# Two more expert steps in the second half's attention of a fused transformer and expert-retrieval block

## The reference

```python
def peer(h, w_q, sub_keys, expert_u, expert_v):
    q = jnp.einsum('bsd,dq->bsq', h, w_q).reshape(b, s_len, PEER_HEADS, 2, PEER_HALF)
    scores = jnp.einsum('bshpc,hpnc->bshpn', q, sub_keys).astype(jnp.float32)
    top_s, top_i = lax.top_k(scores, PEER_TOPK)
    ...
    best_s, best_pos = lax.top_k(cand_s, PEER_TOPK)
    best_i = jnp.take_along_axis(cand_i, best_pos, axis=-1)
    gate = jax.nn.softmax(best_s, axis=-1)
    ...
    def token_block(args):
        xb, ib, gb = args                      # 128 tokens, 128 experts each
        u = jnp.take(expert_u, ib, axis=0)
        act = jax.nn.gelu(jnp.einsum('td,tkd->tk', xb, u).astype(jnp.float32), approximate=False)
        vv = jnp.take(expert_v, ib, axis=0)
        return jnp.einsum('tk,tkd->td', (gb * act).astype(h.dtype), vv)
```

## Time and profile before

| | us |
|---|---|
| runs: lowest, median, highest | 2656.35, 2659.87, 3085.62 |
| profiled execution: time | 2648.0 |
| profiled execution: span of the core | 2646.3 |
| busy: PE, DVE, ACT, POOL | 2158.7, 1726.1, 659.7, 796.3 |

### The profile page before, as it was taken

The page is one execution under the profiler, slowest core; times in us unless marked ns, Lnnn a source line. Parts: engine busy times, 40 slices in busy tenths (PEclk is TensorE's granted clock), DMA queues, the critical chain, the costliest instruction groups (busy, mean ns, idle before and its releaser), DMA issues. The chain is left out here.

```text
span 2646.3 us, 26290 instructions
## 1 busy us (share of the span) xinstructions
PE 2158.7 (82%) x9024; PEld 1622.4 (61%) x9024; DVE 1726.1 (65%) x3624; ACT 659.7 (25%) x1537; POOL 796.3 (30%) x541
## 2 busy tenths in 40 slices
PE   8999999999999999998999988988555554544554
PEld 6787788888778777777888867877111211211221
DVE  4662110002327679687787676667999999999987
ACT  2103212102332421662320234532111111111110
POOL 0000000000001244234443322225754655645642
PEclk9999999999999999999999998889776777778776
DMA  6774334443245699798999974578999999999997
GB/s 256 289 286 130 135 112 159 146 157 116 97 170 225 268 381 419 261 332 344 415 421 412 400 267 176 191 269 328 422 421 422 421 421 421 421 395 421 421 422 298
DMA packets 114868, 798.33 MB, mean 302 GB/s; under 512 B 13328, under 2 KB 16528, under 8 KB 19248
## 3 DMA queue, kind: packets, MB, share of 16 engines
q0 software_dynamic: 74736, 540.57, 50.2%
q1 hardware_dynamic: 40000, 256.09, 26.3%
HBM read 790.27 MB, written 6.34 MB: 301 GB/s over the span
## 5 line engine op out<-in xcount | busy, mean ns | idle before, releaser
L588 PE MATMUL PS<-reg,ring 128*128 128x256 f32 x6016 | 1350.4, 383 | 28.1 <-ACT reg L1109 6.5
L588 PEld LDWEIGHTS PS<-reg,ring 128*128 128x128 f32 x6016 | 1142.5, 192 | 204.9 <-issue 35.9
L536 POOL DMA_INDIRECT uv<-in_expert_uv,experts x329 | 529.6, 1610 | 1610.6 <-DVE experts L1534 862.1
L1581 DVE SCALAR_TENSOR_TENSOR acc<-uv,coef,acc 128x1024 f32<-128x1024 f32 x261 | 335.3, 1285 | 9.5 <-DVE coef L1564 0.3
L563 PE MATMUL PS<-uv,spare 128*128 128x512 f32 x260 | 177.2, 832 | 169.9 <-ACT spare L1046 169.9
L1552 DVE CUSTOM_DVE_ANT_0 uv<-uv,h_tok 128x1024 f32<-128x1024 f32 x225 | 267.2, 1219 | 30.0 <-DMA uv<-in_expert_uv,experts 29.6
L563 PE MATMUL PS<-reg,spare 128*128 128x512 f32 x212 | 140.8, 814 | 118.6 <-ACT spare L1046 118.6
L563 PEld LDWEIGHTS PS<-uv,spare 128*128 128x128 f32 x260 | 64.9, 265 | 278.1 <-issue 278.1
L1053 ACT ACTIVATE acts<-dots 128x2 f32<-128x2 f32 (+2 forms) x194 | 39.4, 203 | 745.5 <-DVE dots L1552 689.2
L536 POOL DMA_INDIRECT reg<-in_expert_uv,experts x107 | 150.3, 1405 | 110.1 <-PE PS L563 39.9
L563 PEld LDWEIGHTS PS<-reg,spare 128*128 128x128 f32 x212 | 51.9, 259 | 206.3 <-issue 206.3
(11 more groups left out here) (265 smaller groups left out, 2102.4 us busy)
## 6 DMA issues: line engine op xcount, KB each, us to landing
ring<-in_weights SPq DMA_DIRECT2D x228, 1024.0 KB, 5.5
uv<-in_expert_uv,experts POOLq DMA_INDIRECT x329, 15.2
kv_half<-reg SPq DMA_DIRECT2D x1, 2052.0 KB, 11.1
reg<-kv_half SPq DMA_DIRECT2D x1, 2052.0 KB, 15.5
reg<-in_x_t SPq DMA_DIRECT2D x2, 1024.0 KB, 4.9
reg<-in_sub_t SPq DMA_DIRECT2D x2, 1024.0 KB, 5.0
toep<-rel_neg SPq DMA_DIRECT2D x16, 128.0 KB, 6.7
x_tokens<-reg SPq DMA_DIRECT2D x2, 1024.0 KB, 10.3
```

The lines of the kernel that those rows point to most:

```text
L536: gp.indirect_dma_start(UV[r], None, a["expert_uv_2"], bass.IndirectOffsetOnAxis(ap=experts[:, e % 256:e % 256 + 1], axis=0))\
L588: mm = pe.matmul(out_tile(n, t), w[:, t * P:(t + 1) * P], mv, start=first and k == 0, stop=last and k == KT - 1)
L1581: dve.scalar_tensor_tensor(acc[:, :], v, c, acc[:, :], ALU.mult, ALU.add).then_inc(acc_done, 1)
```

## The change

Two numbers are added to `MORE`, 6 and 14. A step (two slots) now also stands behind fill tile 6 (the seventh GC tile, item 10) and fill tile 14 (the seventh CP tile, item 20). `FIRST_PE` and `WIDE` move from 198 and 204 to 202 and 208. `STEPS`, the number of steps ahead of the tail, follows: from 99 to 101. The first slot of the tail is 202 instead of 198, and PE accumulates 152 slots instead of 154.

```diff
-FIRST_PE = 198
+FIRST_PE = 202
...
-NUV0, NUV1, WIDE = 7, 17, 204
+NUV0, NUV1, WIDE = 7, 17, 208
...
-MORE = (2, 10, 18)
+MORE = (2, 6, 10, 14, 18)
```

## The result

The changed kernel took 2672.02 us (median of 8 runs, lowest 2663.33), the kernel before 2657.0 beside it (lowest 2647.66). One run of each, 3809.62 and 3085.62 us, was slow (the first at a granted clock of 0.549) and is not in the ratio. The ratio is 1.0057, 95% interval 1.0039 to 1.0075: a loss of about 15 us, between 10 and 20, against a forecast of +10.5. The profiled execution took 2668.49 us with a span of 2666.7, 20.4 longer than before.

What follows compares the result with a forecast made beforehand. It took PE, with DMA nearly full, to bound the stretch from 1215 to 1500 us and gathers the tail. Terms -10.0, +10.3, +6.9, +3.3 gave +10.5: 2658.5 against 2648.0, 2670 on the median, range 2650 to 2688.

Steps and rivals of the forecast that it cites:

- Tail, -10.0: Tail, paced by the gathers: two steps are four slots less at 2.49 us each, -10.0 us.
- Attention, +10.3: Second half's attention: late combines behind tiles 6 (4.3) and 14 (6.5), less 2.5 for a moved routing, plus 2.0 clock; +10.3 us.
- Ahead of WO, +6.9: Attention projection's end: a routing now behind AP1 delays merges WO waits for; 5.4 us more waiting, 1.5 clock; +6.9 us.
- UP2 and UP10 at nothing: Routings landing at UP2 and UP10: PE's evacuations are ACT's and PE waits for nothing there; 0 us.
- DN10, +1: Routing ahead of the residual at DN10: up to 3.5 us late, but PE is late by then; +1 us.
- Mixers, +3.6: Mixers: a routing arrives ahead of the last mLSTM product, where PE already waits 3.69 us; +3.6, between 0 and 5.6.
- -1.3: WO2: a routing leaves it, behind which PE waits 2.59 us; -1.3 us, between 0 and -2.6.
- Q2 to V2, nothing: Stretch from Q2 to V2: no change in length, 0 us.
- The attention absorbs the steps: Rival, chance 0.22: DVE's 44.5 us idle takes the steps; attention +2, projection +4, tail -10; -4 us in all.
- The backlog grows: Rival, chance 0.13: DVE does not catch up between clusters; attention +19, projection +8, others +6, tail -7.5; +26 us.
- The clock stays low: Rival, chance 0.02: stalls keep PE at the lower rate for most of the attention; +59 us there, over 2% slower.
- A table switch holds ACT longer than its load: Rival, chance 0.03: four added switches each hold ACT 1.28 us more; attention 5.1 us more, +15.6 in all.

Runs made afterwards that it cites:

- the spread version: Changed kernel with routings of items 3 to 5 ahead of the attention, 6 behind AP3, 7 to 13 spread over UP1 to UP14, DN4 and Q20; ratio 0.9945.
- DN10's routing moved: Changed kernel with item 10's routing moved two steps later, from behind DN10 to behind Q20; ratio to the kernel before 1.0015.
- the kernel before with a free attention: Kernel before, no step added, with the routings of items 3, 4 and 5 moved out of the attention (V12, V13, XC0); ratio 0.997.
- AP's routing back: Changed kernel with only item 6's routing back at its old place, behind AP3 instead of AP1; ratio to the kernel before 1.0038.
- the routings moved in the kernel before: Kernel before, no step added, with the routings of items 6 to 13 two steps earlier, as in the changed kernel; ratio 1.0037.

## Why the prediction was right, and where not

The forecast was a small loss, +10.5 us; measured are +10 to +20, with 15 in the middle. The tail, the attention's length and the merge ahead of WO came as forecast, and they carry the answer. That the total is so close is partly luck: DN came out 9.65 us above its term and the mixers 7.45 below theirs, and the two nearly cancel. The median's 2670 against 2672.02 is luck too, as the kernel before ran at 2657.0 beside it and not at 2659.87. The forecast took 2% for about what a measurement can tell; the interval here is 0.36% wide. By its own steps:

- **Tail, -10.0: right.** -10.7 in the changed kernel, and -5.6 for one step. The gathers at 2.49 us each give 5.0 a step; what the rest is isn't shown.
- **Attention, +10.3: right as a sum (+10.5), its parts less so.** The waits at tiles 10 and 17 came as named (4.89 and 5.32 us). But alone, tile 6 costs 6.8 (4.3 and a share of the clock forecast) and tile 14 3.2 (6.5 - 2.5 and a share), the latter with no wait for tile 15's combine at all. The routing's move within the attention, reckoned as a cost at one tile and a gain at another, is worth 0.5 us. Adding up late combines follows one chain of many; DVE's added busy time, 9.6 us, comes as near for both steps together.
- **Ahead of WO, +6.9: right**: 5.2 of wait and 1.9 of clock, +7.1.
- **UP2 and UP10 at nothing: right**, as the spread version shows: five routings in UP and one at DN4, where the kernel before has two and one, add 1.2 us to the stretch. DN2's routing, for which the sum has no term, costs no wait either.
- **DN10, +1: the mis-sized term**, +10.65. The step that failed is "PE is late by then and the DMA engines have used that". Being late to UP gave DVE no lead. Relative to PE the additions would have come 1.2 us late at DN11 with no routing ahead of them, and with it moved away PE still waits 1.45 us. The term took 5.6 - 2.05 as its upper bound, 3.5. The wait is 7.64 because the routing's 5.5 us come on top of those 1.2, and because ACT's squares, 0.93 us between the additions and the mean, were left out. Left out as well was the slow clock behind the wait: PE's busy time in the stretch is 3.0 us longer (227.98 against 224.97), which with the 7.64 us makes the whole 10.65. As to why DVE has no lead, only an estimate can be given. In AP and WO the gathers and weights moved 23.1 MB before (28.87 us at 323 GB/s, 33.62 at 409) and 24.3 after (34.08 at 331, 35.56 at 365): 1.2 MB more in 7.1 us that could have carried 3.0 at 421 GB/s, perhaps as the buffers are freed by the steps that the routing holds up. In UP and DN a block with its step then asks for three times 1.0486 MB, 7.47 us at 421 GB/s, and PE's 32 records of a block for 27.89 / 4 = 6.97, so a small lead would be used up there. No run tests this.
- **Mixers, +3.6: wrong in sign, and small.** The last L1968 wait rose from 3.69 to 5.49, not to 7.3. The wait of 11.40 us became 3.42 + 5.90. These nearly cancel (-0.3): PE is idle for as long as before (18.6 against 18.5 us) but busy for 4.0 us less, at a granted clock of 0.90 against 0.87. So the -3.85 is the clock's, which is treated below, and its sign is chance as far as the forecast goes. Behind them the wait of 2.59 us at 1765.27 is gone as a whole: -2.5, within the bounds given for -1.3.
- **Q2 to V2, nothing: +2.1**, all of it PE's busy time (70.10 against 68.01 us, at a granted clock of 0.94 against 0.96); it was not in the sum. That it comes from the DN wait isn't shown: the stretch is 78.3 with a DN wait of 1.45 us and 78.4 in the kernel before with a free attention, which has the order and the waits of before from AP on.

*The attention absorbs the steps* falls: the two steps are 9.6 us of DVE's work and the attention is 10.5 longer. *The backlog grows* falls as a story of the attention, which grew by 10.5 and not 19. *The clock stays low* falls: the granted clock of the attention went from 0.94 to 0.91. *A table switch holds ACT longer than its load* falls too. Two switches at the new DN10 routing, on ACT in order of time in the kernel after:

```profile
1507.77 0.20 ACT L1053 ACTIVATE acts<-dots 128x2 f32<-128x2 f32 x1 [7.22 <-DVE dots L1552]
...
1516.01 0.20 ACT L1053 ACTIVATE acts<-dots 128x2 f32<-128x2 f32 x1 [8.04 <-DVE dots L1552]
1516.23 1.28 ACT L1061 ACT_TABLE_LOAD   x1
...
1527.52 1.28 ACT L1053 ACT_TABLE_LOAD   x1 [4.95 <-DVE dots L1552]
1528.81 0.20 ACT L1053 ACTIVATE acts<-dots 128x2 f32<-128x2 f32 x1
1529.03 1.28 ACT L1089 ACT_TABLE_LOAD   x1
```

The load starts 0.02 us behind the end of an instruction and the next begins 1.29 us after the load began. The Trainium skill (ScalarE: Activation LUTs, What ACT_TABLE_LOAD costs) has a drain of 1.38 us beside the load. The trace does not agree: there is room for 0.03 us here (0.02 ahead of the load, 0.01 behind it), and the attention came out at +10.5, not at the +15.8 that the drain would give.

## What to carry to other kernels

In the stream of an engine that works in order, a long item of background work costs by what stands right behind it and by the lead that the engine has there. The same 5.6 us cost next to nothing behind UP's blocks and ahead of DN3's residual, and 7 to 9 us ahead of the AP merges and of DN11's residual, where DVE had no lead left. When a change adds a few steps, look first at everything that a counter moves with them. Before adding work to a stretch, compare versions of it with more and less work: here DVE was busy 72% of the attention, and work added to it or taken from it still changed the length by 0.7 to 1.4 times as much.

## What was not expected of the hardware

**The clock moves the mixers by 6 us, with the same order and the same waits.** After and DN10's routing moved have the same program there and the same waits of PE (5.90, 1.68, 1.67 or 1.68, and 5.49 us), yet the stretch is 138.5 and 144.6 us. Busy time from the second L1951 wait on, after, and then with DN10's routing moved:

```profile
1668.00:1760.00 92.00, 82.60 (x453) 73.32 (x454) 67.23 (x109) 52.77 (x87) 26.04 (x14) 0.93 0.56 212
```

```profile
1659.00:1757.00 98.00, 88.42 (x450) 77.25 (x451) 67.50 (x109) 52.37 (x86) 26.05 (x14) 0.87 0.53 198
```

PE's 450 records take 82.6 us at a granted clock of 0.93 or 88.4 at 0.87, a different mix of the 1.2 and 2.4 GHz levels. With AP's routing back the stretch is 138.6, with the routings moved in the kernel before 144.5. The two short ones have a long wait at DN11's residual ahead of them (7.64 and 5.47 us), the two long ones a short one (1.45 and 2.39); whether one brings the other isn't shown by four profiles. With the old order of the mixers, six profiles agree within 0.1 us (142.2 to 142.35). So a change of 6 us in this stretch can't be put down to the order by one profile.

**A wait of several us cost about 0.4 of its length again by the clock.** Behind the 7.64 us wait at 1522.29 PE needed 3.0 us more for the rest of DN (granted clock of the stretch 0.98 against 1.00); behind 5.2 us more of waiting ahead of WO it was 1.9 up to UP, with PE's busy time 33.94 against 31.61 us (0.93 against 1.00).
